# A three-layer block on one core: the second rotary attention's scores over 64 rows, two blocks at a time

## What is computed

```python
def windowed_gqa(h, w_qkv, w_o, sinks, cos, sin):      # 16 query heads, 4 kv heads, head width 64, WINDOW 128
    q, k, v = jnp.split(h @ w_qkv, [Hq * d, Hq * d + Hkv * d], axis=-1)
    q, k = apply_rope(q), apply_rope(k)
    s = jnp.einsum('bnqhgd,bnchd->bnhgqc', q, kb) * (d ** -0.5)
    s = jnp.where(|kpos - qpos| <= WINDOW, s, -inf)
    m = jnp.maximum(jnp.max(s, axis=-1, keepdims=True), sink)
    e = jnp.exp(s - m)
    pr = e / (jnp.sum(e, axis=-1, keepdims=True) + jnp.exp(sink - m))
    o = jnp.einsum('bnhgqc,bnchd->bnqhgd', pr, vb)
    return o @ w_o
...
h = h + mix
h = h + conv_ffn(rms_norm(h, ffn_norm[i]), ...)
gate = jax.nn.sigmoid(rms_norm(h, ple_norm[i]) @ ple_w_gate[i])
h = h + (p[i] @ ple_w_proj[i]) * gate
```

## Time and profile before

| | us |
|---|---|
| median of 3 runs | 1076.44 (1075.25 to 1076.63) |
| the profiled execution's own time | 1077.12 |
| its span | 1075.4 |
| TensorE busy (share of the span) | 1058.1 (98%) |
| VectorE busy | 728.9 (68%) |
| ScalarE busy | 589.2 (55%) |
| POOL busy | 92.1 (9%) |
| stretch of the second attention, TensorE's first score load to the first product behind the last block | 387.63 to 450.83 |

### The profile page before, as it was taken

One profiled execution on the slowest core, in us unless ns is written; L12 is line 12 of the kernel. 1 busy time (PEld: TensorE's weight loads), 2 busy tenths in 40 slices (PEclk: granted clock), 3 DMA queues, 4 the chain that ended last, 5 costly groups with the idle time before them and its releaser, 6 DMA issues.

```text
span 1075.4 us, 17488 instructions
## 1 busy us (share of the span) xinstructions
PE 1058.1 (98%) x6920; PEld 956.3 (89%) x6920; DVE 728.9 (68%) x997; ACT 589.2 (55%) x893; POOL 92.1 (9%) x150
## 2 busy tenths in 40 slices
PE   8899999999999999999999999999999999999997
PEld 7788899999998887899999998899899989998996
DVE  5976677877777855477787777866655586555553
ACT  5766765555546757565564556734433566434442
POOL 1311110000000243210000000401000000000000
PEclk9999999999999999999999999999999999999999
DMA  8633345566554441345555545564353356565531
GB/s 292 221 120 128 118 157 175 181 228 199 158 194 152 162 144 53 118 159 174 194 197 195 196 157 186 176 189 156 115 160 121 123 179 215 167 198 192 186 126 40
DMA packets 114644, 177.51 MB, mean 165 GB/s; under 512 B 3419, under 2 KB 85524, under 8 KB 114580
## 3 DMA queue, kind: packets, MB, share of 16 engines
q1 hardware_dynamic: 114004, 175.05, 49.3%
q10 hardware_dynamic: 576, 1.57, 0.4%
HBM read 175.56 MB, written 1.05 MB: 164 GB/s over the span
## 4 chain that ended last, share of the span: by engine, by line
PE 89%; ACT 5%; SPq 2%; issue 2%; DVE 1%; POOL 1%; DMA 1%; POOLq 0%; ACTq 0%; DVEq 0%
PE ps L1803 85%; PE ps L1877 1%; DMA raw<-in_diff_w_qkv 1%; ACT whi L682 1%; ACT scr L854 1%; ACT whi L670 1%; POOL scr L575 1%; PE ps L1923 1%; PE ps L2046 1%; PE ps L2268 0%; PE ps L2391 0%; SPq L436 0%; ACT scr L706 0%; ACT scr L1084 0%; ACT scr L908 0%
## 5 line engine op out<-in xcount | busy, mean ns | idle before, releaser
L1190 DVE TENSOR_TENSOR wlo<-raw,whi 128x2048 fp32r<-128x2048 f32 x149 | 341.3, 2296 | 79.7 <-ACT whi L670 78.3
L1803 PE MATMUL ps<-xhi,whi 128*128 128x256 f32 x1248 | 355.2, 285 | 0.0
L1803 PE MATMUL ps<-xlo,whi 128*128 128x256 f32 x1248 | 353.1, 283 | 0.0
L1803 PE MATMUL ps<-xhi,wlo 128*128 128x256 f32 x1248 | 353.1, 283 | 0.0
L670 ACT ACTIVATE whi<-raw 128x2048 fp32r<-128x2048 f32 x149 | 282.8, 1909 | 53.1 <-PE ps L1803 34.3
L1803 PEld LDWEIGHTS ps<-xhi,whi 128*128 128x128 f32 x1248 | 239.2, 192 | 3.9 <-issue 1.4
L1803 PEld LDWEIGHTS ps<-xlo,whi 128*128 128x128 f32 x1248 | 239.3, 192 | 1.2
L1803 PEld LDWEIGHTS ps<-xhi,wlo 128*128 128x128 f32 x1248 | 239.3, 192 | 0.0
L806 ACT ACTIVATE scr<-scr,cwT 128x256 f32<-128x256 f32 x88 | 48.1, 594 | 142.3 <-DVE scr L1333 142.3
L1803 PE MATMUL ps<-whi,ohi 128*128 128x512 f32 x368 | 124.8, 397 | 0.0
L1803 PE MATMUL ps<-whi,olo 128*128 128x512 f32 x368 | 122.2, 390 | 0.0
(11 more groups left out here) (188 smaller groups left out, 1141.2 us busy)
## 6 DMA issues: line engine op xcount, KB each, us to landing
raw<-in_ffn_w_up SPq DMA_DIRECT2D x44, 1024.0 KB, 5.1
raw<-in_w_in SPq DMA_DIRECT2D x23, 1024.0 KB, 5.3
raw<-in_ffn_w_down SPq DMA_DIRECT2D x22, 1024.0 KB, 5.0
raw<-in_w_mlp_in SPq DMA_DIRECT2D x16, 1024.0 KB, 5.3
raw<-in_w_mlp_out SPq DMA_DIRECT2D x16, 1024.0 KB, 4.9
raw<-in_diff_w_qkv SPq DMA_DIRECT2D x11, 1024.0 KB, 6.3
raw<-in_ple_w_gate SPq DMA_DIRECT2D x8, 1024.0 KB, 4.9
raw<-in_swa_w_qkv SPq DMA_DIRECT2D x6, 1024.0 KB, 5.5
```

What stands on the lines that cost most here:

```text
L1190: dve.tensor_tensor(wlo[:, u % RING, :], raw[:, u % RAW, :], whi[:, u % RING, :].bitcast(F32), ALU.subtract).then_inc(lo_ready, 1)
L1803: return pe.matmul(o, l, r, start=start, stop=stop, skip_group_check=True)
```

## The change

Scores are computed over 64 rows. `copy_qs` copies a transposed query tile whole, with one instruction, into `qS`, and a score matmul takes the 64 rows of its head from `qS` and `kT`. `SWA_BLOCKS` is reordered so that two blocks that differ only in their row half follow each other, and `scores1(s)`, called for even s, issues both: for each j the matmul of row half 0 into bank 6 and that of row half 1 into bank 7, then the two masks. It waits for the exponentials of the two blocks before it. All the loops go over pairs. POOL no longer zeroes `qT` in this layer. Both sink exponentials of a pair stand behind the first probability copy on ScalarE; a half split stands between the two copies. The transposes of the second query group move from s = 4 and 6 to 2 and 6, those of outputs from s = 5, 9, 13 to 4, 8, 12. `PP_BANK` of layer 1 becomes (0, 2), with the waits that belong to it. The number of half splits stays 10; the last are placed otherwise.

```diff
--- before.py
+++ after.py
@@ -189,6 +189,7 @@
 
 
         qT = region(0, 2048, "p (r a c) -> p r a c", r=2, c=SEQ)
+        qS = region(0, 2048, "p (a c) -> p a c", c=SEQ)
         kT = region(2048, 2048, "p (a c) -> p a c", c=SEQ)
         vtm = region(4096, 2048, "p (t c) -> p t c", t=T)
         rotA = region(6144, 1024, "p (t c) -> p t c", t=T)
@@ -380,7 +381,7 @@
         BLOCKS = [(qt, i) for qt in range(2) for i in range(4)]
         N_A = 8
 
-        SWA_BLOCKS = [(g, qt, r, 2 * ip) for g in range(2) for qt in range(2) for r in range(2) for ip in range(2)]
+        SWA_BLOCKS = [(g, qt, r, 2 * ip) for g in range(2) for qt in range(2) for ip in range(2) for r in range(2)]
 
 
         T_ORDER = [f"0{name}{t}" for name in ("q0", "k0") for t in range(T)]
@@ -392,14 +393,14 @@
         T_ORDER += [f"1{name}{t}" for name in ("k", "q0") for t in range(T)]
         for s in range(2 * N_A):
             T_ORDER.append(f"1A{s}")
-            if s in (4, 6):
-                T_ORDER.append(f"1q1{s // 2 - 2}")
+            if s in (3, 7):
+                T_ORDER.append(f"1q1{(s - 3) // 4}")
         T_ORDER += [f"2S{s}" for s in range(8)]
         for s, (j, qt) in enumerate(DIL_BLOCKS):
             T_ORDER += [f"2D{s}a", f"2D{s}b"][0:qt + 1]
         T_USE = {name: n for n, name in enumerate(T_ORDER)}
 
-        PP_BANK = ((0, 2), (2, 0))
+        PP_BANK = ((0, 2), (0, 2))
 
         TB, OB = 4, 5
 
@@ -602,8 +603,6 @@
                 norm_rstd(1)
                 norm_rstd(2)
                 norm_rstd(3)
-                pool.wait_ge(hlo_ready[0], FT // 2)
-                zero_other_heads()
                 for c, w in ((4, 256), (5, HALF)):
                     for t in range(T):
                         rope_add(c, t, w)
@@ -624,8 +623,8 @@
                     pool.wait_ge(sinkexp_ready, s + 1)
                     settle(pool.tensor_tensor(esum1[:, s], esum1[:, s], sinkd[:, s], ALU.add))
                     pool.tensor_tensor(rsum1[:, s], esum1[:, s], minus1, ALU.pow).then_inc(sum_ready, 1)
-                    if s in (1, 3):
-                        rope_add(6, s // 2, HALF)
+                    if s in (1, 2):
+                        rope_add(6, s - 1, HALF)
                 norm_rstd(4)
                 norm_rstd(5)
                 norm_rstd(6)
@@ -898,6 +897,9 @@
 
                 def copy_k(tiles, t):
                     copy_T(kT[:, tiles, t * P:(t + 1) * P], ps[:, TB, :].rearrange("p (a c) -> p a c", c=P)[:, 0:tiles.stop - tiles.start, :])
+
+                def copy_qs(tiles, t):
+                    copy_T(qS[:, tiles, t * P:(t + 1) * P], ps[:, TB, :].rearrange("p (a c) -> p a c", c=P), 0.125)
 
                 def copy_q(t, zeroed):
 
@@ -993,7 +995,7 @@
                 ahead(u + 2)
                 copy_k(slice(0, 2), 1)
                 for t in range(T):
-                    copy_q(t, 2)
+                    copy_qs(slice(0, 4), t)
                 ahead(u + 3)
 
                 def swa_exp(s):
@@ -1008,22 +1010,28 @@
                     act.wait_ge(sinkarg_ready, s + 1)
                     act.activation(sinkd[:, s], sinkd[:, s], ACT.Exp).then_inc(sinkexp_ready, 1)
 
-                swa_exp(0)
-                sink_exp(0)
-                for s in range(2 * N_A):
-                    if s + 1 < 2 * N_A:
-                        swa_exp(s + 1)
-                    copy_T(ATs[:, s % 2].rearrange("p k c -> p (k c)"), ps[:, TB, :])
-                    if s in (5, 9, 13):
-                        o_hi(*((0, 4, 4, 0), (0, 4, 5, 1), (4, 4, 6, 0))[(s - 5) // 4], False)
-                    if s + 1 < 2 * N_A:
-                        sink_exp(s + 1)
-                    if s in (4, 6):
-                        copy_q(s // 2 - 2, 2)
+                for s in range(2):
+                    swa_exp(s)
+                for s in range(0, 2 * N_A, 2):
+                    more = s + 2 < 2 * N_A
+                    copy_T(ATs[:, 0].rearrange("p k c -> p (k c)"), ps[:, TB, :])
+                    sink_exp(s)
+                    sink_exp(s + 1)
+                    if more:
+                        split_half()
+                    copy_T(ATs[:, 1].rearrange("p k c -> p (k c)"), ps[:, TB, :])
+                    if more:
+                        swa_exp(s + 2)
+                        swa_exp(s + 3)
+                    else:
+                        split_half(2)
+                    if s in (4, 8, 12):
+                        o_hi(*((0, 4, 4, 0), (0, 4, 5, 1), (4, 4, 6, 0))[(s - 4) // 4], False)
+                    if s in (2, 6):
+                        copy_qs(slice(4, 8), (s - 2) // 4)
                     if s in (4, 6):
                         ple_proj(1, s // 2 - 2)
-                    if s % 4 in (0, 1) or s > 13:
-                        split_half()
+                split_half()
                 o_hi(4, 4, 7, 1, False)
                 ahead(U0["wo1"] + 2)
                 act.dma_start(gmid, final_norm.partition_broadcast(P)).then_inc(gmid_loaded, 16)
@@ -1575,21 +1583,19 @@
                 swa_max(0)
                 swa_max(1)
                 ahead(u + 3)
-                for s in range(2 * N_A):
-                    if s % 4 in (1, 2):
-                        split_half()
-                    if s:
-                        swa_out(s - 1)
+                for s in range(0, 2 * N_A, 2):
                     if s + 2 < 2 * N_A:
                         swa_max(s + 2)
-                    if s in (5, 9, 13):
-                        o_lo(*((0, 4, 4, 0), (0, 4, 5, 1), (4, 4, 6, 0))[(s - 5) // 4], False)
-                    if s in (1, 3):
-                        rope_mul(6, s // 2, "qkv1.2", U0["qkv1"] + 5, 0, 8)
-                    if s == 15:
-                        split_half()
-                swa_out(2 * N_A - 1)
-                split_half()
+                        swa_max(s + 3)
+                    swa_out(s)
+                    split_half()
+                    if s in (4, 8, 12):
+                        o_lo(*((0, 4, 4, 0), (0, 4, 5, 1), (4, 4, 6, 0))[(s - 4) // 4], False)
+                    swa_out(s + 1)
+                    if s == 0:
+                        for t in range(T):
+                            rope_mul(6, t, "qkv1.2", U0["qkv1"] + 5, 0, 8)
+                split_half(2)
                 o_lo(4, 4, 7, 1, False)
                 boundary(lambda t, hf: residual("wo1", U0["wo1"] + 3, t, hf), 4, second=(U0["wo1"] + 2,))
                 ahead(U0["wo1"] + 3)
@@ -2231,11 +2237,13 @@
                     if s < 2:
                         q1_piece(1, s + 2)
                     elif s < 6:
-                        if s == 4:
+                        if s == 2:
                             pe.wait_ge(rope_read, 14)
                         ple_piece(1, s - 2)
                     elif 7 <= s < 15:
                         if s == 7:
+                            pe.wait_ge(pp_ready, 6)
+                        if s == 11:
                             pe.wait_ge(pp_ready, 8)
                         if s in (7, 11):
                             pe.wait_ge(olo_ready, 5 + s // 11)
@@ -2246,18 +2254,22 @@
                         (o_read, S_AT["1"] + 8 * st + 4 * qt + 4))
 
                 def scores1(s):
-                    g, qt, r, i = SWA_BLOCKS[s]
+                    g, qt, _, i = SWA_BLOCKS[s]
                     if s == 0:
                         pe.wait_ge(t_free, T_USE["1q01"] + 1)
                         pe.wait_ge(rope_read, 12)
                     if s in (8, 12):
                         pe.wait_ge(t_free, T_USE[f"1q1{s // 4 - 2}"] + 1)
+                    pe.wait_ge(exp_ready, S_AT["1"] + s)
                     c = (1 - qt) * P
-                    pair = ps[:, 6 + s % 2, :].rearrange("p (j c) -> p j c", j=2)
+                    pair = [ps[:, 6 + r, :].rearrange("p (j c) -> p j c", j=2) for r in range(2)]
                     for j in range(2):
-                        mm(pair[:, j, :], qT[:, r, i + j, qt * P:(qt + 1) * P], kT[:, g, :], j == 0, False)
-                    mm(pair[:, :, c:c + P], identb[:, :], maskb[:, qt, :].unsqueeze(1).broadcast_to([P, 2, P]), False, True)\
-                        .then_inc(s_ready, 1)
+                        for r in range(2):
+                            rows_ = slice(r * HD, (r + 1) * HD)
+                            mm(pair[r][:, j, :], qS[rows_, 4 * g + i + j, qt * P:(qt + 1) * P], kT[rows_, g, :], j == 0, False)
+                    for r in range(2):
+                        mm(pair[r][:, :, c:c + P], identb[:, :], maskb[:, qt, :].unsqueeze(1).broadcast_to([P, 2, P]), False, True)\
+                            .then_inc(s_ready, 1)
 
                 def probs_T1(s):
                     t_begin(f"1A{s}")
@@ -2280,20 +2292,24 @@
                     ins.then_inc(o_ready, 1)
 
                 scores1(0)
-                scores1(1)
                 q1_piece(1, 1)
-                for s in range(2 * N_A):
+                for s in range(0, 2 * N_A, 2):
+                    last = s + 2 == 2 * N_A
```

(22 more changed lines are left out.)

## The result

The changed kernel took 1070.72 us (median of 5, 1069.73 to 1071.32) against 1076.56 beside it: a ratio of 0.9945, interval 0.9934 to 0.9956, 5.8 us. 1071.4 was forecast, 1069.0 to 1075.2 the range. TensorE is still the bound.

The account below looks back on a forecast made before the run. TensorE was taken as the bound. Scores 3.8, order 1.0 and query copies 0.1 made 4.9, rounded to 5.0 us: 1077.12 to 1072.1 profiled, 1071.4 us as the median, range 1069.0 to 1075.2.

Parts of the forecast that it names:

- The scores: Second attention on TensorE: 64-row score instructions in alternate halves, 1.49 us a pair against 1.96; 3.8 us gained for eight.
- The entry: Four transposes ahead of a pair's 64-row scores on TensorE: 0.11 us more than the usual 0.43.
- The order: Order of pairs on TensorE in the second attention: waits of 2.4 us against 3.4, 1.0 us gained.
- The tail: End of second attention: last low half done 0.4 us before the fourth remaining piece; costed at 0, 0.5 if cover goes.
- The rest: Queries copied in one instruction, 0.1 us sooner; POOL's zeroing, bank swap and SP's transfers 0.
- Open loads: Rival: each of a half's four score instructions shows its load, 0.10 us; 0.19 more a pair, 1072.9 us; chance 0.21.
- Free ends: Rival: a pair's score instructions overlap with no cost at the ends; 0.41 more gained a pair, 1068.1 us; chance 0.07.
- Hand-offs: Rival: ScalarE's list between probability copies delays second copy or exponentials, 0.45 us a pair; 1075.0 us, no change; chance 0.13.
- Serial halves: Rival: row halves of the scores run one after another, 1.99 us a pair for 1.06; 1078.9 us; chance 0.09.

Follow-up runs that it names:

- the experiment: The changed kernel's order of pairs, but each score matmul over all 128 rows from zero-padded query planes, as before: 1074.9 us, ratio 0.9988.
- the run in one half: Changed kernel with pairs made of two blocks of the same row half, so all eight 64-row instructions use one half: 1077.36 us, ratio 1.0016.

## Why the prediction was right

- **The scores.** Forecast 1.06 us for the eight instructions, measured 1.07. The reading behind it, streaming side by side plus a fixed 0.21, is now shown from two sides: 1.93 us for eight in one half is 1.71 + 0.22, and 1.07 is 0.85 + 0.22. The entry is 0.10 (0.11 was forecast). The term was still short by a fifth, 3.8 for 4.9, in two places. The 0.10 for a load in the open behind the visit isn't there: the masks stand directly behind and take their 0.22, so a pair costs 1.39 us, not 1.49. And the first two visits, which follow a pause, gained 0.76 us each against full height (1.07 for the 1.83 of the experiment's 385.67 to 387.50): at full height a pause opens 0.10 of a load, while a 64-row visit pays its 0.22 in any case. Six visits at 0.56 and two at 0.76 are the 4.9.
- **The order.** Forecast 1.0, measured 0.90. The waits that are left were forecast as 2.4 us and are 2.36 from start to start: 0.79 and 0.29 at the start (0.8 and 0.3), 0.53 at blocks 6 and 7 (0.6), 0.75 at the last pair (0.6). At blocks 6 and 7 the size was right and the reason wrong: the query transposes were to wait for ScalarE's copy, but they lost only 0.04, and the values behind them waited for VectorE (L1579). Those on the low halves went. The pair of 6.9 us was 6.82, with outputs 7.27 for 7.3.
- **The tail.** Its cover was said to be 0.4 us. VectorE's timeline:

```profile
447.39 0.69 DVE L1424 TENSOR_TENSOR olo<-ps,ohi 128x512 fp32r<-128x512 f32 x1
```

The last low half ends at 448.08, and the fourth remaining piece starts at 449.03: 0.95 us of cover. Costed at nothing, and nothing it was.
- **The rest.** The query copies gave 0.08, ahead of the stretch (from the transposes of the first query tile to the first scores 3.75 us, 383.20 to 386.95, where it was 3.82, 383.81 to 387.63; 0.1 was forecast); the bank swap, the zeroing and the transfers nothing that a wait shows.
- **The rivals.** Open loads (1072.9): refused, by the visit of 1.07 us and by the run in one half. Free ends (1068.1): refused, the 0.22 is paid in each visit and the 0.10 ahead of each that follows without a pause; only the 0.10 behind the visit, a quarter of what this rival left out, isn't there. Hand-offs (1075.0): refused, 1.3 us more a pair on ScalarE make the stretch only 1.4 us longer. Serial halves: the one-half run is what that rival would have been, 1077.4 against the 1078.9 worked out for it. That price used 0.249 for each instruction, where the cost is one fixed 0.22 a visit.

The sum was 5.0, and the stretch gave 5.8: 4.9 + 0.9, with the sizes above. The miss of 0.8 us is in the scores; no two errors had to cancel for the time to come out.

## What to carry over

A matmul of half the rows saves nothing by itself, and here costs a fixed 0.22 us a visit and 0.10 at its entry; it pays when the other half of the array has work at the same time, and the more in one visit the better, since the fixed part is paid once. Price such a form from another place of the same kernel at two sizes: the difference is the streaming, the rest is the fixed part. When a wait at one place is filled, look at the queue places of the other engines first: here one on POOL and one on VectorE took back 0.9 of the 1.2 us that filling it gave, and mending POOL's alone returned 0.14.

## What was not expected of the hardware

Eight instructions in two row halves take 1.07 us in alternating order and 1.07 us with four of the one half ahead of four of the other. The section "The mechanism" in Part 3 of "TensorE: Matmul & The Clock Gate" in the Trainium skill says that matmuls start and end strictly in program order; starts in that order would have made the second at least 1.49 us (0.64 + 0.85, as instructions of one half are 0.21 apart), and its second start is 0.01 us behind the first. This run doesn't bear the rule out; whether the ends keep the order, no run here shows.
